# Two key branches of sparse attention as one run of 64 steps, their gate features computed between the steps, SiLU as a tangent on ScalarE and a product on VectorE

## The reference, cut to what matters

```python
def _nsa_layer(x, attend, norm_pre, w_in, w_out, norm_post):
    p = _rmsnorm(x, norm_pre) @ w_in
    q = p[..., :B_ATT]                                # 16 heads of 64
    z = p[..., B_ATT:4 * B_ATT].reshape(bsz, s, 3, B_ATT)
    g = jax.nn.sigmoid(p[..., 4 * B_ATT:])            # one gate per branch and head
    o = attend(q)                                     # branches: compressed, selected, window
    y = (o * g[..., None]).reshape(bsz, s, 3, B_ATT) * jax.nn.silu(z)
    y = jnp.sum(y, axis=2) @ w_out
    return x + _rmsnorm(y, norm_post)
```

## Time and profile before

| | |
|---|---|
| median of 3 runs | 1610.75 us |
| the profiled execution, its own time | 1615.93 us |
| its span | 1614.2 us |
| PE busy | 1450.1 us (90%) |
| DVE busy | 664.2 us (41%) |
| ACT busy | 468.0 us (29%) |
| mean granted clock of PE, in shares of full speed | 0.941 |

### The profile page before, as it was taken

One profiled execution on the slowest core, in us unless ns is written; L12 is line 12 of the kernel. 1 busy time (PEld: TensorE's weight loads), 2 busy tenths in 40 slices (PEclk: granted clock), 3 DMA queues, 4 the chain that ended last, 5 costly groups with the idle time before them and its releaser, 6 DMA issues. The chain is left out here.

```text
span 1614.2 us, 24207 instructions
## 1 busy us (share of the span) xinstructions
PE 1450.1 (90%) x9493; PEld 1071.2 (66%) x9493; DVE 664.2 (41%) x1338; ACT 468.0 (29%) x1126; POOL 171.2 (11%) x229
## 2 busy tenths in 40 slices
PE   6999499999997499997995999999999798988977
PEld 5887365656553399776774999886676454755555
DVE  1544334665655632536423231014202564046546
ACT  4111132333331322434322221221002342134433
POOL 4000040303030000000103110100000000000010
PEclk9999689999998799998997999988999899999989
DMA  6110025766777622314924240030232321231121
GB/s 175 53 53 0 6 85 185 230 230 228 230 254 237 252 68 91 120 53 160 311 86 134 90 165 6 5 105 17 97 102 69 96 58 58 53 105 76 39 72 56
DMA packets 92742, 182.01 MB, mean 113 GB/s; under 512 B 10023, under 2 KB 24003, under 8 KB 91427
## 3 DMA queue, kind: packets, MB, share of 16 engines
q1 hardware_dynamic: 89382, 163.76, 30.7%
q0 software_dynamic: 3248, 16.72, 3.2%
HBM read 133.82 MB, written 54.95 MB: 117 GB/s over the span
## 5 line engine op out<-in xcount | busy, mean ns | idle before, releaser
L1934 PE MATMUL ps<-xnT,wring 128*64 128x256 f32 (+1 forms) x1536 | 180.0, 398 | 4.4 <-PEq L2573 3.0
L1934 PEld LDWEIGHTS ps<-xnT,wring 128*64 128x64 f32 x1536 | 126.4, 139 | 58.0 <-issue 7.4
L367 PE MATMUL ps<-xnT,wring 128*128 128x288 f32 (+1 forms) x512 | 122.1, 400 | 1.1 <-PEq L2728 1.1
L962 DVE SCALAR_TENSOR_TENSOR wring<-wring,nbw,ps 128x512 f32<-128x512 f32 x128 | 87.0, 741 | 65.7 <-PE ps L672 65.6
L367 PEld LDWEIGHTS ps<-xnT,wring 128*128 128x128 f32 x512 | 99.0, 195 | 21.2 <-ACT xnT L287 1.2
L2346 ACT ACTIVATE P<-ps,nmx 128x128 f32<-128x128 f32 (+3 forms) x128 | 66.3, 523 | 101.1 <-DVE nmx L2374 100.9
L1307 PE MATMUL ps<-wh,xl 128*128 128x512 f32 x224 | 89.2, 398 | 0.0
L1138 PE MATMUL ps<-xh,wh 128*128 128x256 f32 (+1 forms) x256 | 74.7, 292 | 11.1 <-DVE wl L1171 11.1
L2374 DVE TENSOR_REDUCE nmx<-ps 128x1 f32<-128x128 f32 (+3 forms) x128 | 56.7, 485 | 62.0 <-PE ps L2223 57.3
L1139 PE MATMUL ps<-xl,wh 128*128 128x256 f32 (+1 forms) x256 | 74.2, 290 | 0.0
L1140 PE MATMUL ps<-xh,wl 128*128 128x256 f32 (+1 forms) x256 | 73.8, 288 | 0.0
(11 more groups left out here) (462 smaller groups left out, 2825.8 us busy)
## 6 DMA issues: line engine op xcount, KB each, us to landing
wring<-in_state_C_dram SPq DMA_DIRECT2D x32, 1024.0 KB, 6.2
out_dram<-wring SPq DMA_DIRECT2D x32, 1024.0 KB, 8.1
wring<-in_a_w_up_dram SPq DMA_DIRECT2D x8, 2048.0 KB, 8.6
wring<-in_b_w_in_dram SPq DMA_DIRECT2D x8, 2048.0 KB, 8.6
wring<-in_a_w_down_dram SPq DMA_DIRECT2D x4, 2048.0 KB, 8.5
craw<-in_cache_kv_dram SPq DMA_DIRECT2D x64, 128.0 KB
arena<-in_cache_kv_dram SPq DMA_DIRECT2D x32, 256.0 KB, 3.8
arena<-in_cache_win_dram SPq DMA_DIRECT2D x8, 1024.0 KB, 5.9
```

The source lines that it names most:

```text
L367: m = pe.matmul(b[:, 0:t1 - t0], w[:, kt, 128 * m4:128 * m4 + 128], k.xnT[:, kt, t0:t1], start=kt == 0, stop=kt == KD - 1)
L962: dve.scalar_tensor_tensor(out=c, in0=c, scalar=nbws[:, h % 2, 2 * S + s:2 * S + s + 1], in1=b[:, :], op0=ALU.mult, op1=ALU.add).then_inc( ...
L1934: m = pe.matmul(b[64 * par:64 * par + 64, 0:t1 - t0], w[:, kt, x:x + DH], k.xnT[:, kt, t0:t1], start=kt == 0, stop=kt == KD - 1)
```

## The change

The two calls of `stage_key_branch` become one call of `stage_keys`: one block, one program per engine, with 64 pairs (v, i, gp, hh) where v is the branch less one. The units' order is now v, gp, i (before: i, gp within a branch). Of the 32 banks of gate features only the first 8 (branch 1, first half) come ahead of the steps; the other 24 stand one in each even step from 0 to 46, between the samples' work and the transposes T. ACT takes each of these banks with tanh(z/2) into one buffer (`zt`, which lies over masks that are no longer needed), and DVE multiplies (tanh + 1) by the bank; the half that is missing is put into the gates `k.gt` at the start of the block. The bank is let go by DVE. The turning of the samples' rows stands in steps 10 and 46, the loads of weights behind the loads of cached rows, and POOL gates the first key branch's samples between its units 8 and 9.

```diff
-        for br in (1, 2):
-            with ExitStack() as c:
-                stage_key_branch(nc, k, c, br)
+        with ExitStack() as c:
+            stage_keys(nc, k, c)
...
-    units = [(i, gp) for i in range(NT) for gp in range(2)]
+    units = [(v, i, gp) for v in range(2) for gp in range(2) for i in range(NT)]
+    ROWS_BACK = {10: 0, 46: 1}
+    GATED_AT = 9
+    def gates_at(n):
+        if n % 2 or n >= 3 * NP // 4:
+            return None
+        c, m = n // (2 * 2 * HPG) + 1, n // 2 % (2 * HPG)
+        return (1 + c // 2, c % 2, m), max(0, 4 * (c - 2) + (2 if m < HPG else 4)) if c > 1 else 0
...
     def _(pe):
-        z_features(pe, k, br, 0)
-        z_features(pe, k, br, 1)
-        turn_samples(pe, k, br - 1)
+        z_features(pe, k, 1, 0)
         for n in range(STEPS):
+            if n in ROWS_BACK:
+                turn_samples(pe, k, ROWS_BACK[n])
...
+            if gates_at(n) is not None:
+                z_bank(pe, k, *gates_at(n)[0])
             if TURN <= n < NP + TURN:
...
     def _(sp):
+        fetch_samples(sp, k, 0)
+        for q in range(2 * NQ):
+            if q:
+                bank, n = k.bank_of[("sO", q - 1)]
                 sp.wait_ge(k.bank_full[bank], n)
...
+            if q in (1, 3, 5, 7):
+                c = CH_IN + 5 + NW + q // 2
+                load_chunks(sp, k, c, c + 1)
+            if q == NQ:
+                store_rows(0)
+                bank, n = k.bank_of[("osT", 0)]
+                sp.wait_ge(k.bank_full[bank], n)
+                fetch_samples(sp, k, 1)
...
     def _(act):
-        z_silu(act, k, br, 0)
-        z_silu(act, k, br, 1)
+        def tangent(br, c, m, no):
+            if no:
+                act.wait_ge(k.gate_done, no)
+            b, _ = full_bank(act, k, ("z", br, HPG * c + m % HPG, m // HPG))
+            w = 256 + S * (m // HPG)
+            act.activation(zt[:, 0:w], b[:, 0:w], ACT.Tanh, scale=0.5).then_inc(k.gate_exp, 1)
...
     def _(dve):
+        def gate(br, c, m, no):
+            t, hf = HPG * c + m % HPG, m // HPG
+            w = 256 + S * hf
+            dve.wait_ge(k.gate_exp, no + 1)
+            b, free = full_bank(dve, k, ("z", br, t, hf))
+            if hf:
+                dve.scalar_tensor_tensor(out=k.zs[:, br % 2, t, :], in0=zt[:, 256:w], scalar=1.0, in1=b[:, 256:w],
+                                         op0=ALU.add, op1=ALU.mult)
+            st.then(dve.scalar_tensor_tensor(out=k.z[:, t, 256 * hf:256 * hf + 256], in0=zt[:, 0:256], scalar=1.0, in1=b[:, 0:256],
+                                             op0=ALU.add, op1=ALU.mult))
+            dve.sem_inc(free, 1)
+            dve.sem_inc(k.gate_done, 1)
...
+        st.then(dve.tensor_scalar(k.gt[:, 0:NT, H:3 * H], k.gt[:, 0:NT, H:3 * H], 0.5, None, ALU.mult))
...
             if TURN <= n < NP + TURN:
                 keep(dve, n - TURN, 0)
+            if gates_at(n) is not None:
+                gate(*gates_at(n)[0], 2 * HPG + n // 2)
```

More of the change, by code:

```diff
@@ L1922, in _, with z_bank, z_silu_bank @@
         dve.memset(k.QS[:, :, :, :], 0.0).then_inc(k.q_clear, 1)
-def z_features(pe, k, br, c):
[L1927 to L1937, removed]
-def z_silu(act, k, br, c):
[L1941 to L1947, removed]
+def z_bank(pe, k, br, c, n):
+    w = chunk(pe, k, CH_IN + 3 + 2 * br + c)
+    hh, hf = n % HPG, n // HPG
+    t0, t1 = HALF[hf]
+    b, full = open_bank(pe, k, ("z", br, HPG * c + hh, hf))
+    for kt in range(KD):
+        for par in range(2):
+            x = 256 * par + DH * hh
+            m = pe.matmul(b[64 * par:64 * par + 64, 0:t1 - t0], w[:, kt, x:x + DH], k.xnT[:, kt, t0:t1],
+                          start=kt == 0, stop=kt == KD - 1)
+    m.then_inc(full, 1)
+    k.chunk_last[CH_IN + 3 + 2 * br + c] = k.bank_of[("z", br, HPG * c + hh, hf)]
+def z_features(pe, k, br, c):
+    for n in range(2 * HPG):
+        z_bank(pe, k, br, c, n)
+def z_silu_bank(act, k, br, c, n):
+    t, hf = HPG * c + n % HPG, n // HPG
+    b, free = full_bank(act, k, ("z", br, t, hf))
+    m = act.activation(k.z[:, t, 256 * hf:256 * hf + 256], b[:, 0:256], ACT.Silu)
+    if hf:
+        m = act.activation(k.zs[:, br % 2, t, :], b[:, 256:288], ACT.Silu)
+    m.then_inc(free, 1)
+def z_silu(act, k, br, c):
+    for n in range(2 * HPG):
+        z_silu_bank(act, k, br, c, n)
 def z_ready(eng, k, br, c):
@@ L2263, in _ @@
                 m.then_inc(full, 1)
-                b, full = open_bank(pe, k, ("sTn", br, s))
+                b, full = open_bank(pe, k, ("sTn", q))
                 pe.transpose(b[0:S, 0:128], sP[:, T:TA], k.ident[:, :]).then_inc(full, 1)
[L2266 to L2270, removed]
+            q = two(n, VALUES)
+            if q is not None:
+                drained(pe, k, ("sT", q))
+                drained(pe, k, ("sTn", q))
+                b, full = open_bank(pe, k, ("sO", q))
                 both = b[:, 0:2 * DH].rearrange("p (a d) -> p a d", a=2)
@@ L2311, in _ @@
     def _(sp):
[L2312 to L2317, removed]
-                sp.wait_ge(k.bank_full[bank], n)
[L2319 to L2325, removed]
@@ L2331, in _ @@
+        store_rows(1)
     @block.scalar
     def _(act):
-        z_silu(act, k, br, 0)
-        z_silu(act, k, br, 1)
+        def tangent(br, c, m, no):
[4 more added lines that the diff above has]
+            act.activation(zt[:, 0:w], b[:, 0:w], ACT.Tanh, scale=0.5).then_inc(k.gate_exp, 1)
+        for m in range(2 * HPG):
+            tangent(1, 0, m, m)
@@ L2400, in out @@
             dve.sem_inc(k.o_free, 1)
-        z_ready(dve, k, br, 0)
-        z_ready(dve, k, br, 1)
+        st.then(dve.tensor_scalar(k.gt[:, 0:NT, H:3 * H], k.gt[:, 0:NT, H:3 * H], 0.5, None, ALU.mult))
+        st.then(dve.tensor_scalar(k.gt[0:S, NT, H:3 * H], k.gt[0:S, NT, H:3 * H], 0.5, None, ALU.mult))
+        dve.sem_inc(k.gt_halved, 1)
+        for m in range(2 * HPG):
+            gate(1, 0, m, m)
         for n in range(STEPS + 1):
+            if n in ROWS_BACK:
+                add_samples(dve, k, st, ROWS_BACK[n])
             if n < NP:
@@ L2423, in _ @@
                 st.then(dve.tensor_reduce(out=snmx[:, 1:2], in_=b[:, 0:S], axis=AX.X, op=ALU.max))
                 dve.tensor_reduce(out=snmx[:, 2:3], in_=snmx[:, 0:2], axis=AX.X, op=ALU.max, negate=True).then_inc(k.mx_ready, 1)
-            s = two(n, TURNS)
-            if s is not None:
-                if s:
-                    bank, c = k.bank_of[("sO", br, s - 1)]
+            q = two(n, TURNS)
+            if q is not None:
+                if q:
+                    bank, c = k.bank_of[("sO", q - 1)]
@@ L2454, in _ @@
     def _(pool):
-        gate_samples(pool, k, br - 1)
-        for u, (i, gp) in enumerate(units):
-            pool.wait_ge(k.o_free, ADDED + u + 1)
+        gate_samples(pool, k, 0)
+        for u, (v, i, gp) in enumerate(units):
+            if u == GATED_AT:
+                pool.wait_ge(k.gt_halved, 1)
+                gate_samples(pool, k, 1)
+            pool.wait_ge(k.o_free, u + 1)
             rows = k.y[:, HPG * gp:HPG * gp + HPG, 128 * i:128 * i + 128]
             pool.tensor_tensor(rows, rows, tmp[:, u % 2, :].rearrange("p (h q) -> p h q", h=HPG), ALU.add).then_inc(k.added, 1)
-            pool.wait_ge(k.added, ADDED + u + 1)
-    k.maxima += 2 * NP + NQ
+            pool.wait_ge(k.added, u + 1)
 def stage_out(nc, k, ctx):
```

183 lines of the change are left out of this document (99 added, 84 removed).

## The result

On the chip of the prediction the changed kernel took 1584.6 us (median of 4, 1581.37 to 1587.38) and the kernel before 1610.38 us (median of 4): ratio 0.9824, interval 0.9804 to 0.9845, 25.8 us less. The forecast was 1586.3 us. On another chip the same pair gave 1583.08 (5 runs) and 1613.94 us (23 runs, 1606.56 to 1619.89), ratio 0.9811, 0.9779 to 0.9843. The two profiled executions, 1615.93 and 1584.48 us, lie 31.4 us apart; their spans are 1614.2 and 1582.8 us.

A forecast was written before the change was run, and what follows sets the result against it. PE was taken to bound both branches, with some 32 us idle in the steps and a lowered clock. 5.8 + 5.9 + 6.5 + 7.2 - 1.0 = 24.4 us off 1610.75 gave 1586.3 us, range 1576 to 1599 (8 in 10).

The forecast's parts named there:

- Seam: Between the branches: last exponential, row weights and block's end come to lie beside other work, 5.8 us won.
- cached rows: Branch 1: banks of features between give the loads time, so PE's waits for cached rows go, 5.9 us won.
- waits of the first 48 steps: Steps 0 to 47: features cover even steps' waits, odd steps keep 6.2 of 12.7 us, 6.5 us won.
- The last 16 steps: End of branch 2: without features there, they keep 6.0 us of waits and the waits at the end.
- The clock: PE in the steps: 7.2 us won as the clock comes back, with 0 and 10.8 us as the ends.
- I take two thirds: Clock term: of 10.8 us short of full speed, 7.2 us counted, since part falls on idle time already counted.
- Branch 2's 0.94 I leave: Clock term: no gain counted for branch 2's steps, since half stay without features and the end stays too.
- What is added: Costs of changing places on PE, tangent on ACT and product on DVE: 1.0 us together, near the lower ends.
- the hand-overs: PE's matmuls change places 48 times more: 3.4 us if each overlap of about 0.07 us were lost, lower end nothing.
- The clock stays a mix: Rival: short waits left in the steps hold the clock down, the 7.2 us stay away: 1593.5 us, chance 0.09.
- The bank's way through two engines: Rival: PE stands still for tangent and product, at most 1.55 us in each of 24 steps: 1624 us, chance 0.04.
- Only the seam: Rival: each step keeps its waits and clock, only the 5.8 us between the branches are won: 1605 us, chance 0.02.

The follow-up runs named there:

- e1_bursts: Changed kernel with its 24 banks of gate features in bursts of eight at steps 0, 32 and 40, products ahead of the copy of T: 1593.88 us.
- e7_odd: Changed kernel with the 24 banks in the odd steps 1 to 47 instead of the even ones: 1613.91 us, ratio 1.0002 to the kernel before.
- e8_spread: Changed kernel with banks at steps 0, 3, 4 of each eight in all 64 steps, DVE asking only for the half it reads: 1577.4 us.
- e3_double: Changed kernel with DVE's product of the gate features done twice for each bank: 1590.17 us, ratio 0.9841 to the kernel before.
- e6_order: Kernel before with only the order of units in a branch changed to gp, i: 1608.27 us, ratio 0.9962 to the kernel before.
- e2_silu: Changed kernel with SiLU as one ACT function instead of tangent on ACT and product on DVE: 1605.55 us, ratio 0.9945 to the kernel before.

## Why the prediction was right, step by step

*Seam, cached rows, waits of the first 48 steps*: right by place and size. 5.8 and 5.9 us are gone; behind the scores of odd steps 6.4 us are left where 6.2 were forecast, and none behind those of the even ones in the first 48. Idle time fell by 19.2 us; the three terms say 18.2. e1_bursts brings the waits back, e7_odd moves them, e8_spread removes those that the change leaves.

*The last 16 steps*: waits right (6.3 us for 6.0, the ends as before), clock not: it was 1.00 there too.

*The clock* is the term that was mis-sized: 7.2 us forecast, about 17 us measured. The earlier trace rows put it 8.9 + 1.9 + 7.4 = 18.2 us short of full speed by means of two digits, narrow windows around the falls add up to 17.1 us, and after nothing is short. Two choices failed. "I take two thirds", because part of the shortfall would fall on idle time: behind the long waits PE is busy for the whole time at the lower level, as these 6 us windows of the kernel before show, which begin with the matmuls behind a wait (the second is that of the earlier trace rows):

```profile
1472.78:1478.78 6.00, 6.00 (x34) 0.72 0.00 1
1504.36:1510.36 6.00, 6.00 (x32) 0.72 0.00 0
```

A wait that brings the lower clock is thus paid with 1.7 us more, nearly in full. Seven such places lie in what the change removed (two waits for cached rows, two for exponentials in branch 1, its row weights, the seam, and the 2.03 us ahead of 1472.78): 7 * 1.7 = 11.9 us. The other choice was "Branch 2's 0.94 I leave": one of the seven is there, and about 5 us more lie at two waits of the last 16 steps that are still waited for, and were not followed by the lower clock this time: 1.7 us behind the wait of the earlier trace rows, 3.4 us at the last row weights. The windows of 8 us with a PEclk below 1.00 from 1500 to 1548 (us, PE busy, PEclk, DMA, GB/s) are three:

```profile
1500.00:1508.00 8.00, 5.87 (x34) 0.79 0.00 0
1532.00:1540.00 8.00, 5.18 (x32) 0.92 0.00 0
1540.00:1548.00 8.00, 7.16 (x32) 0.65 0.00 0
```

That last part is not shown to be the change's doing. The lower clock came after them in e3_double, and after the last row weights in e8_spread.

Side by side, the shortfall goes with the number of gaps of 2 us and more rather than with the idle time of the stretch: 17.1 us with eight gaps and 35.2 us idle (before), 15.4 with eight and 32.2 (e7_odd), 12.0 with five and 32.3 (e6_order), 5.1 with two and 33.2 (e2_silu), 1.7 with three and 27.1 (e1_bursts). The new order of units, which the forecast put at nothing because it leaves every width as often, alone took away 5.1 us of it in e6_order.

*What is added*: 1.0 us forecast. 12.8 us less busy time, with 17.1 us from the clock, leaves about 4 us more work on PE. The nearest view of it: a bank in the middle of the steps, from its first matmul to the scores behind it,

```profile
1205.05 3.67 PE L1934 MATMUL ps<-xnT,wring 128*64 128x256 f32 x32
...
1208.65 0.49 PE L2240 MATMUL ps<-KT,Qp 64*128 64x128 f32 x4
```

takes 3.60 us, and a bank of the same width in the opening burst 3.45 to 3.5, by the operations of ACT that follow each bank:

```profile
1181.28 0.38 ACT L2371 ACTIVATE masks<-ps 128x256 f32<-128x256 f32 x1 [3.13 <-PE ps L1934]
1184.73 0.38 ACT L2371 ACTIVATE masks<-ps 128x256 f32<-128x256 f32 x1 [3.07 <-PE ps L1934]
```

24 times 0.10 to 0.15 us are 2.4 to 3.6 us: the upper end of the hand-overs, 3.4 us, was the right one, not the lower. The product went as thought: 416 ns for the wide form, just under the lower bound, and 180 ns for the narrow one, hidden in its place (groups of DVE):

```profile
L2426 DVE SCALAR_TENSOR_TENSOR z<-masks,ps 128x256 f32<-128x256 f32 x32 | 13.3, 416 | 15.7 <-ACT masks L2371 15.7
...
L2424 DVE SCALAR_TENSOR_TENSOR zs<-masks,ps 128x32 f32<-128x32 f32 x16 | 2.9, 180 | 13.6 <-ACT masks L2371 13.6
```

*The whole.* By the profiles the stretch won 32.0 us where 24.4 (372.7 to 348) were forecast: the clock 9.9 us more, the idle time 1.0 us more, the added work some 3 us more. The median of the first chip moved by 25.8 us only, with four runs on each side; on the second it was 30.9. That the forecast time met 1584.6 so closely is in part luck: two of its terms were off in opposite directions, and the low median of before, 1610.75, was its start, while by the stretch the gain was 7.6 us larger than the forecast one. The waits were right for the reason given; the size of the whole was not.

*The rivals.* "The clock stays a mix" is out: 19 waits, 17 of them of 0.25 to 0.75 us, and 1.00. The Trainium skill, TensorE: Matmul & The Clock Gate, section "A second HAM failure mode: psum-queue depth-cycling", ties such swings, in another kernel, to frequent small gaps between groups; the trace of the kernel after, with these 19 waits for exponentials at 1.00, does not agree; e7_odd, with 16 such waits but longer ones, has the lower level (1.2 GHz) behind nine of its 14 gaps of 1 us and more. "The bank's way through two engines" is out: no wait for a product. "Only the seam" is out by the waits.

**Left open.** In the ten profiles, the steps have 41 gaps of PE of 2 us and more; the lower clock followed 32 of them, all eight in each profile of the kernel before, four of five in e6_order, one of three in e1_bursts, none of two in each profile of the kernel after. What decides it was not settled, and with it not how much of the last 16 steps' 5 us and of e6_order's gain would stay in another kernel.

## What to carry to other kernels

Work that waits for nothing is worth most right behind the scores whose exponential the next step needs, with its own follow-up out of the way of the next maxima: with 24 banks of features there the kernel took 1583 us, with the same banks in three bursts 1594, and with each of them one step later 1614, as before the change. Count a long wait of TensorE twice where the trace shows the lower clock behind it, once as idle time and once, nearly in full, as the shortfall in the window that follows. Before two functions of ScalarE are made to alternate, read in the trace what the table loads between them take; here 2.6 us a pair would have eaten most of the gain.

## What the runs showed that was not expected

- Behind a wait that brings the lower clock, 6 us windows had 0.72 again and again (1472.78, 1504.36 before; 1481.84 in e3_double): the same 1.7 us, though not everywhere; at the last row weights it was 3.4 us before and in e3_double and e8_spread.
- The same wait, 2.03 to 2.07 us in the same step, was followed by 0.72 in one kernel and 1.00 in another.
- The order of units alone moved the kernel before by 5.7 us (e6_order), mostly by the clock.
- 23 runs of one unchanged kernel on one chip lay between 1606.56 and 1619.89 us, 0.8% apart, and the 5 us between two profiled executions lay in stages ahead of the changed one.
- Tangent and Exp took turns in ACT without one table load between them.
